# Down projection: feature sums split in the first round, differences ahead of low parts, one square per chunk, and an earlier copy of the row sums

## What is computed

```python
merged = ga * (ya @ w_branch_a[i]) + gb * (yb @ w_branch_b[i]) + gc * (yc @ w_branch_c[i])
x = x + rms_norm(merged @ w_out[i], g_mix_post[i])
h2 = rms_norm(x, g_ffn_pre[i])
u = causal_dwconv(h2 @ w_up[i], conv_w[i], conv_b[i])
ug, uv = u[..., :D_FF], u[..., D_FF:]
f = (jax.nn.gelu(ug, approximate=True) * uv) @ w_down[i]
x = x + rms_norm(f, g_ffn_post[i])
pg = jax.nn.sigmoid(rms_norm(x, g_ple_pre[i]) @ w_ple_gate[i])
x = x + rms_norm(pg * (p[i] @ w_ple[i]), g_ple_post[i])
```

## Time and profile before

| | |
|---|---|
| median of 3 runs | 1868.92 us (1868.49 to 1871.56) |
| the profiled execution | 1870.65 us, its span 1868.8 us |
| PE, matmuls | 1825.6 us busy, 98% of the span |
| DVE | 1175.5 us, 63% |
| ACT | 935.3 us, 50% |
| POOL | 320.6 us, 17% |
| granted clock of PE, mean | 0.989 of full |
| HBM read and written | 145 GB/s over the span |

### The profile page before, as it was taken

How to read it: one execution, slowest core, us unless ns; L and a number is a source line. 1 busy time by engine, 2 the same in 40 slices (tenths; PEclk the granted TensorE clock), 3 DMA queues, 4 the chain that set the end, 5 groups by cost and what they waited for, 6 DMA issues and landing times.

```text
span 1868.8 us, 26896 instructions
## 1 busy us (share of the span) xinstructions
PE 1825.6 (98%) x9111; PEld 1511.3 (81%) x9111; DVE 1175.5 (63%) x1804; ACT 935.3 (50%) x1660; POOL 320.6 (17%) x314
## 2 busy tenths in 40 slices
PE   9999999999999999898999999999989999999988
PEld 8888888787888888776898888887878888887777
DVE  4756555544577777777656555555436777778775
ACT  4676546632454444454547764565235444444453
POOL 1002001232013333101010020012310233331010
PEclk9999999999999999998999999999999999999999
DMA  6322354478323333675253234446762333337742
GB/s 182 83 83 80 108 103 128 115 197 225 102 88 117 107 118 107 226 263 168 93 152 92 58 91 108 96 130 150 196 202 80 110 107 115 118 118 234 249 148 90
DMA packets 311144, 249.23 MB, mean 133 GB/s; under 512 B 65092, under 2 KB 265440, under 8 KB 310752
## 3 DMA queue, kind: packets, MB, share of 16 engines
q1 hardware_dynamic: 301160, 222.51, 39.8%
q0 software_dynamic: 9504, 25.17, 6.3%
q10 hardware_dynamic: 376, 0.21, 0.1%
HBM read 232.57 MB, written 38.27 MB: 145 GB/s over the span
## 4 chain that ended last, share of the span: by engine, by line
PE 61%; DVE 13%; issue 9%; ACT 7%; DMA 6%; POOL 1%; ACTq 1%; DVEq 1%; POOLq 0%; SPq 0%
PE psum L886 51%; DMA col_sums<-in_w_down_dram 4%; ACT wh L1512 3%; PE psum L1201 2%; DVE cg L2428 2%; PE psum L1182 2%; DVE cg L2430 2%; PE psum L1167 2%; ACT cg L1740 2%; DVE ft_both L2430 2%; DVE ft_both L2428 2%; DVE ft_both L2437 2%; DMA row_sums<-in_w_down_dram 1%; ACT ft_both L1740 1%; PE psum L929 1%
## 5 line engine op out<-in xcount | busy, mean ns | idle before, releaser
L886 PE MATMUL psum<-xnh,wh 128*128 128x512 f32 (+1 forms) x1424 | 566.2, 398 | 0.0
L886 PE MATMUL psum<-xnh,wl 128*128 128x512 f32 (+1 forms) x1424 | 549.5, 386 | 0.0
L886 PE MATMUL psum<-xnl,wh 128*128 128x512 f32 (+1 forms) x1424 | 548.8, 385 | 0.0
L1968 DVE TENSOR_TENSOR wl<-raw,wh 128x1024 fp32r<-128x1024 f32 (+2 forms) x276 | 368.7, 1337 | 237.5 <-ACT wh L1512 237.3
L1512 ACT ACTIVATE wh<-raw 128x1024 fp32r<-128x1024 f32 (+2 forms) x276 | 283.2, 1026 | 235.3 <-PE psum L886 178.6
L886 PEld LDWEIGHTS psum<-xnh,wh 128*128 128x128 f32 x1424 | 269.2, 189 | 54.7 <-issue 5.8
L886 PEld LDWEIGHTS psum<-xnh,wl 128*128 128x128 f32 x1424 | 267.7, 188 | 54.6
L886 PEld LDWEIGHTS psum<-xnl,wh 128*128 128x128 f32 x1424 | 268.5, 189 | 46.1
L2203 DVE CUSTOM_DVE_ANT_0 Sp<-psum,ptok 128x128 f32<-128x128 f32 (+3 forms) x128 | 62.7, 491 | 108.6 <-issue 60.8
L1744 ACT ACTIVATE cg<-cg 128x512 f32<-128x512 f32 x44 | 27.8, 633 | 128.7 <-DVE cg L2430 128.7
L1748 ACT ACTIVATE fh<-ft_both 128x256 f32 (+1 forms) x44 | 18.4, 418 | 143.8 <-DVE ft_both L2437 143.8
(11 more groups left out here) (333 smaller groups left out, 3500.3 us busy)
## 6 DMA issues: line engine op xcount, KB each, us to landing
raw<-in_w_up_dram SPq DMA_DIRECT2D x88, 512.0 KB, 3.8
raw<-in_w_gate_dram SPq DMA_DIRECT2D x48, 512.0 KB, 3.8
col_sums<-in_w_down_dram POOLq DMA_DIRECT2D x44, 512.0 KB, 7.0
raw<-in_w_down_dram SPq DMA_DIRECT2D x44, 512.0 KB, 4.5
raw<-in_w_in_dram SPq DMA_DIRECT2D x30, 512.0 KB, 3.7
raw<-col_sums SPq DMA_DIRECT2D x22, 512.0 KB, 4.6
raw<-in_w_down_dram SPq DMA_DIRECT2D x40, 256.0 KB, 4.0
qspill<-f_sums SPq DMA_DIRECT2D x22, 384.0 KB, 4.8
```

The lines of the kernel that those rows point to most:

```text
L886: ins = pe.matmul(out, left, right, start=start and n == 0, stop=stop and n == 2)
L1968: dve.tensor_tensor(low[:, 0:n], raw[(L * NCH + c) % RAW][:, 0:n], hi[:, 0:n].bitcast(F32), ALU.subtract).then_inc(w_lo.sem, 1)
```

## The change

It has five parts. The eleven feature sums are split in the first round (`Q_PREP` 5 to 21) through four buffers that lie where the normed input of the up stage was. In the second round `diff` is made one chunk earlier, in front of the low part of `dn_cols`. Chunk 3's parts are made ahead of the last features, and chunk 4's high part ahead of the last cross features. The sums of squares are taken one at a time, at chunks 31, 33, 35 and 37, and the gains at 30, 32, 34 and 36. The copy of the row sums is issued at POOL's turn 0, with its own semaphore `row_copied`.

```diff
-Q_PREP = [2 * j + 8 for j in range(7)] + [26, 28, 30, 32]
+Q_PREP = [5, 7, 9, 10, 12, 13, 15, 16, 18, 19, 21]
+Q_RAW = 4
...
-    q_raw = [here(f"q_raw{i}", 96 + 3 * i, [P, 768]) for i in range(3)]
+    q_raw = [in_xn(f"q_raw{i}", 16 + 3 * i, [P, 768]) for i in range(Q_RAW)]
... SP
                     if c == ST_DOWN + Q_PREP[j]:
                         if j == 0:
-                            wait(f_lo.sem, f_lo.at(L, 3 * PAIRS))
-                        wait(q_spilled.sem, q_spilled.at(L, 16 * PAIRS) if j == 0 else q_spilled.at(L, 16 * (j + 1)))
-                        if j >= 3:
-                            wait(q_lo.sem, q_lo.at(L, j - 2))
-                        sp.dma_start(q_raw[j % 3][:, :], qspill[L, :, j, :]).then_inc(q_back[j % 3].sem, 16)
-                if c == ST_DOWN + 30:
+                            wait(w_used.sem, w_used.at(L, ST_DOWN))
+                        wait(q_spilled.sem, q_spilled.at(L, 16 * (j + 1)))
+                        if j >= Q_RAW:
+                            wait(q_lo.sem, q_lo.at(L, j - Q_RAW + 1))
+                        sp.dma_start(q_raw[j % Q_RAW][:, :], qspill[L, :, j, :]).then_inc(q_back[j % Q_RAW].sem, 16)
+                if c == ST_DOWN + 28:
                     wait(w_used.sem, w_used.at(L, ST_DOWN + 2 * PAIRS))
                     gain_load(L, 1, "g_ffn_post")
... ACT
+                if last:
+                    hi(L, ST_DOWN + 3)
                 act.wait_ge(ft_ready.sem, ft_ready.at(L, s // 2 + 1) + it * 2)
...
-            act.wait_ge(w_used.sem, w_used.at(L, ST_DOWN + 2 * j + 2))
-            act.activation(qh[:, j, :], q_raw[j % 3][:, :], ACT.Copy).then_inc(q_hi.sem, 1)
+            act.wait_ge(w_used.sem, w_used.at(L, ST_DOWN + 2 * ((3 * j + 2) // 4) + 2))
+            act.activation(qh[:, j, :], q_raw[j % Q_RAW][:, :], ACT.Copy).then_inc(q_hi.sem, 1)
...
-            for n in range(3, 4 * PAIRS + 2):
+            for n in range(5, 4 * PAIRS + 2):
                 hi(L, ST_DOWN + n)
...
-                if n == 31:
-                    half_sums(L)
+                if n in (31, 33, 35, 37):
+                    half_sum(L, n // 2 - 15)
...
-            up_post(L, -1, 2 * FT // 4)
+            up_post(L, -1, 2 * FT // 4, last=True)
+            hi(L, ST_DOWN + 4)
             cross_hi(L, PAIRS - 1)
... DVE
+            if a == 0:
+                dve.wait_ge(q_lo.sem, q_lo.at(L, PAIRS))
             dve.wait_ge(p_full.sem, p_full.at(L, 4 + a))
...
+                dve.wait_ge(p_taken.sem, p_taken.at(L, 4))
             dve.tensor_tensor(yg_dn[:, t, cols], ydn[:, t, cols], gain_down[:, cols], ALU.mult)
...
-            for n in range(3, 4 * PAIRS):
+            for n in range(4, 4 * PAIRS):
                 q = n - 2 * PAIRS
-                if q >= 0 and q % 2 == 1:
+                if q >= 0 and q % 2 == 0:
                     diff(L, q // 2)
...
-                if n in (33, 34, 35, 36):
-                    half_gain(L, n - 33)
+                if n in (30, 32, 34, 36):
+                    half_gain(L, n // 2 - 15)
...
                 lo(L, ST_DOWN + 1)
                 lo(L, ST_DOWN + 2)
+                lo(L, ST_DOWN + 3)
... POOL
-            if s > 0:
+            if s == 0:
+                pool.dma_start(row_sums[L], rows[L, 0, :, 0:1]).then_inc(row_copied.sem, 16)
+            if 0 < s <= PAIRS:
                 pool.wait_ge(wsum_copied.sem, wsum_copied.at(L, 16 * s))
-            if 0 < s <= PAIRS:
                 pool.dma_start(col_sums[L, :, pair(s - 1), :], cols[L, 1, :, pair(s - 1), :], max_dma_last_dim=2048,
                                accum_op=ALU.add).then_inc(wsum_in.sem, 16)
             if s == PAIRS + 1:
+                pool.wait_ge(row_copied.sem, row_copied.at(L, 16))
                 pool.dma_start(row_sums[L], rows[L, 1, :, 0:1], max_dma_last_dim=4096, accum_op=ALU.add
                                ).then_inc(wsum_in.sem, 16)
             if s < PAIRS:
                 pool.dma_start(col_sums[L, :, pair(s), :], cols[L, 0, :, pair(s), :]).then_inc(wsum_copied.sem, 16)
-            if s == PAIRS:
-                pool.dma_start(row_sums[L], rows[L, 0, :, 0:1]).then_inc(wsum_copied.sem, 16)
```

More of the change, by code:

```diff
@@ L361, in trunk_kernel @@
     q_spilled = Tally(sem("q_spilled"), 16 * PAIRS, 16)
-    q_back = [Tally(sem(f"q_back{i}"), 16 * len(range(i, PAIRS, 3))) for i in range(3)]
+    q_back = [Tally(sem(f"q_back{i}"), 16 * len(range(i, PAIRS, Q_RAW))) for i in range(Q_RAW)]
     q_hi = Tally(sem("q_hi"), PAIRS)
     q_lo = Tally(sem("q_lo"), PAIRS)
-    wsum_copied = Tally(sem("wsum_copied"), 16 * (PAIRS + 1))
+    wsum_copied = Tally(sem("wsum_copied"), 16 * PAIRS)
+    row_copied = Tally(sem("row_copied"), 16)
     wsum_in = Tally(sem("wsum_in"), 16 * (PAIRS + 1))
@@ L1728, in keys_apart, with up_post @@
             act.activation(kB[0:HD, 2 * j + 1, :], keys_at[j][HD:P, :], ACT.Copy).then_inc(kt_empty.sem, 1)
-        def up_post(L, s, it):
+        def up_post(L, s, it, last=False):
             value, pair = s % 2, (s // 2) % 2
@@ L1757, in sums_hi @@
         def sums_hi(L, j):
-            act.wait_ge(q_back[j % 3].sem, q_back[j % 3].at(L, 16 * (j // 3 + 1)))
-            act.wait_ge(w_used.sem, w_used.at(L, ST_DOWN + 2 * j + 2))
-            act.activation(qh[:, j, :], q_raw[j % 3][:, :], ACT.Copy).then_inc(q_hi.sem, 1)
+            act.wait_ge(q_back[j % Q_RAW].sem, q_back[j % Q_RAW].at(L, 16 * (j // Q_RAW + 1)))
+            act.wait_ge(w_used.sem, w_used.at(L, ST_DOWN + 2 * ((3 * j + 2) // 4) + 2))
+            act.activation(qh[:, j, :], q_raw[j % Q_RAW][:, :], ACT.Copy).then_inc(q_hi.sem, 1)
         def products_out(L):
@@ L1771, in products_out, with half_sum @@
                     act.activation(dst[a][:, :], bank[4 + 2 * k + a], ACT.Copy).then_inc(p_out.sem, 1)
-        def half_sums(L):
-            for i, t in enumerate((0, 1, 2, 3)):
-                act.wait_ge(half_made.sem, half_made.at(L, i + 1))
-                act.wait_ge(half_summed.sem, half_summed.at(L, i))
-                act.activation(sq_dn[0][:, early_half(t)], ydn[:, t, early_half(t)], ACT.Square, scale=YSCALE,
-                               accum_out=ysums[:, 0, t:t + 1]).then_inc(half_summed.sem, 1)
+        def half_sum(L, t):
+            act.wait_ge(half_made.sem, half_made.at(L, t + 1))
+            act.wait_ge(half_summed.sem, half_summed.at(L, t))
+            act.activation(sq_dn[0][:, early_half(t)], ydn[:, t, early_half(t)], ACT.Square, scale=YSCALE,
+                           accum_out=ysums[:, 0, t:t + 1]).then_inc(half_summed.sem, 1)
         def rest_sum(L, i):
@@ L2058, in sums_lo @@
             dve.wait_ge(q_hi.sem, q_hi.at(L, j + 1))
-            dve.tensor_tensor(ql[:, j, :], q_raw[j % 3][:, :], qh[:, j, :].bitcast(F32), ALU.subtract
+            dve.tensor_tensor(ql[:, j, :], q_raw[j % Q_RAW][:, :], qh[:, j, :].bitcast(F32), ALU.subtract
                               ).then_inc(q_lo.sem, 1)
         def threes_taken(L, a):
+            if a == 0:
+                dve.wait_ge(q_lo.sem, q_lo.at(L, PAIRS))
             dve.wait_ge(p_full.sem, p_full.at(L, 4 + a))
```

## The result

The changed kernel takes 1841.76 us, the median of four executions (1841.51 to 1847.50), beside 1869.76 (1868.49 to 1871.56) for the kernel before on the same chip: a ratio of 0.9857, 95% interval 0.9836 to 0.9878. That is 28.0 us less where 38.5 were forecast. The time lies inside the range of 1822 to 1846, but 11.4 us above the forecast of 1830.4 (the kernel before had 1868.92 when the forecast was made), so outside the 5 us around it. The profiled execution of the changed kernel is the slowest of its four: 1847.5 us, span 1845.7. Its span is 23.1 us under that of the profile before.

What follows compares the result with a forecast made beforehand. TensorE (PE) was taken as the bound, busy in 98% of the span. Gains of 14.1 us at the gates, 11.5 in layer 0 and 12.9 in layer 1 made 38.5 off 1868.92: 1830.4 us, range 1822 to 1846.

Steps and rivals of the forecast that it cites:

- (a): First round of down: the loads hold it, landing in 7.2 us; 5.9 us a layer, 1842 in all; chance 0.17.
- (b): Second round of down: it loses through the difference's wait, landings 5.7 us; 5.4 a layer, 1841 in all; chance 0.09.
- the gates: End of the third branch's gates: issuing the row_sums copy at POOL's turn 0 gains 14.1 us, low end 10.
- one of its own signs: Down projection: the prediction is wrong if row sums wait for DMA in most pairs, or if diffs do.
- Turn 11 still waits for the copy of pair 10: POOL's queue at the gates: that copy had landed by 437.15, and PE stood nowhere for it.
- chunk 3 and chunk 4: First round: the 3.33 us stall before chunk 3 goes; a new one of 1.4 us comes before chunk 4.
- From there PE eats a pair in 5.44 us: First round after chunk 4: DVE needs 4.5 us per pair, under PE's 5.44, so no loss.
- the 2.9 of the prediction: First round: loss left in the round, 1.4 + 1.5 us, of 6.2 and 6.6 before.
- three causes that the prediction named: Second round: four fewer low parts of sums on DVE, squares spread out, difference one chunk ahead (0.76 us waited before).
- Low 39 ended T-3.4, load 43 lands T+1.4: Second round's tail, T being when PE ends chunk 37: leads to a 1.9 us stall and 0.2 to restart.
- cycle over two pairs: Second round: DVE's loads and parts take 7.1 to 7.7 us, under PE's 8.16, so no loss.
- the embedding's give-back: Embedding after down: DVE's last additions start later, so 1.8 us a layer comes back as a PE stall.

Runs made afterwards that it cites:

- the yardstick's: The changed kernel run once more without any edit, in the second group, beside the kernel before: 1843.38 us, ratio 0.9857.

## Why the prediction was right, and where it was wrong

The time lies in the range, but near the rivals (a) and (b), at 1842 and 1841 us, and not near the forecast. It is not there for their reasons in full, as shown below: the gates came as forecast, the down projection gained much less, and the embedding's error went the other way and hid 4.7 us of that, which is luck. By one of its own signs the prediction failed: it was to be wrong if differences wait for their loads, and 8 of 11 do in each layer. The row sums do so in 4 and 5 of 10.

**Right: the gates, by mechanism and size.** 14.1 us forecast; 12.6 measured alone. In the profiled execution of the changed kernel 4.4 of them came back in layer 1 through the copy of pair 9; in the yardstick's trace nothing did. The three executions with spans near 1840 are 5.8 us shorter than the profiled one; that this stall is most of what they lack is argued from its size, as they have no trace. The slow matmuls in the first rounds (3.2 us in the profiled execution, none in the yardstick's trace) are another thing that comes and goes. "Turn 11 still waits for the copy of pair 10" was true, but the wait at pair 9 was not looked at in the prediction, and the profile before had left it no effect.

**Right: chunk 3 and chunk 4.** The stall before chunk 3 went as forecast, and chunk 4 loses 0.83 and 0.81 us where 1.4 stood. It is not all new: the profile before shows 1.02 us lost before chunk 4 in layer 0 (769.35), which the prediction did not name.

**Wrong in the first round: the step "From there PE eats a pair in 5.44 us. DVE needs ..., 4.5 us per pair".** It takes undisturbed durations and an average over 17 chunks. The stall that came, 1.98 us at chunk 6, lies right at its beginning, where the first sum's low part (1.49) stands ahead of low 6, and where POOL's last two low parts still slow DVE. The prediction had that slowing down for chunk 4 and dropped it from there on. Two runs show it: with POOL quiet 0.36 is left, with the sum moved nothing is. Behind it a second thing was hidden, SP's spill ahead of loads 8 and 9; with both out of the way the rounds lose 2.5 us each, near the 2.9 of the prediction. Rival (a) is not this: DVE's row sums did wait for loads, PE was not held by them.

**Right in sign, too large in the second round: the regular part.** PE stands nowhere between the rounds' change and chunk 38, as forecast, in the first trace; in the yardstick's it stands 1.54 us once, for a load of 7.7 us. Of the three causes that the prediction named, the difference ahead of time is worth 4.0 to 5.7 us by medians of different groups, of which the trace shows 2.6 as stalls of the ping-pong. The spread squares are worth nothing that can be measured once the rest is in place: the 3.31 us that DVE stood for high 32 would have been filled by a wait for a load. What the four low parts fewer are worth was not tried alone.

**Wrong in the tail: the step "Low 39 ended T-3.4, load 43 lands T+1.4".** T was 844.3. Low 39 ended at 842.65, T-1.7, because load 39, issued at 835.05, landed at 840.2, and each difference now waits for its load. Load 43 then took 5.06 us where 4.8 stood, and landed at T+3.5, not T+1.4. The mis-sized term stands ahead of it, the "cycle over two pairs" of 7.1 to 7.7 us: from one difference to the second after it DVE needed 7.6 to 8.3 us in the last pairs of layer 0 (828.37 to 836.10 is 7.73, 831.93 to 840.22 is 8.29) and 8.0 to 8.6 in layer 1, beside PE's 8.16. So the parts gained nothing on PE on the way, and in the tail three pairs fall due at once. Thus 1.9 us became 0.77 and 3.20, and 2.26 and 3.48 in layer 1, with 1.7 to 1.9 more at the slow clock. That is the tail of rival (b), with its "1.9 if the clock falls there", and at 3.6 and 5.7 us a layer over the forecast it is near (b)'s 5.4. But (b)'s condition, landings of 5.7 us, holds only in part: the loads from 33 on took 4.4 to 5.2 us in layer 0 and 4.9 to 6.0 in layer 1 (load 43 there 6.04), and its 1.5 us in the pairs did not come in this trace.

**Wrong with it: the embedding's give-back.** The 1.8 us per layer needed a PE that is early. As PE is late in the tail, the cover holds and the embedding loses 0.0 and 0.5. Once PE is made earlier, by the shorter tail or the buffers, it loses 3.9 to 7.0 us a layer there, two to four times what was forecast. The mechanism was right, its size too small.

Summed: the gates gained 4.4 us, the first rounds 6.3 and the second rounds 9.4 less than forecast, the embedding 4.7 more: 15.4 less in all for the profiled execution. The median is 11.4 off; that it is less goes with the stall at the gates, which the profiled execution has and the others probably lack. In the yardstick's trace the same account reads otherwise: gates as forecast, first rounds 3.1 and second rounds 14.0 less, embedding 5.2 more. That the second rounds hold most of the miss stands in both.

In two versions every execution is under every one of the changed kernel's, in both of its groups: the later spill with the later split (1840.20), and the one with two more buffers on top of it (1840.17). The first changes a list and one number and is the one to take. It is 3.2 us under the changed kernel of its own group, or 0.2%.

## What to carry to other kernels

When stalls are removed from one engine, ask of each remaining wait on the helpers whether it only becomes visible next: here ping-pong with ACT turned into waits for loads. What the shorter tail or the buffers took off the tail came back in the embedding or at another load, and no version tried here won both. An average rate of work per pair is no proof for the first pairs: work out the first and the last ones one by one, with the durations that hold while the other engines are still busy. And an in-order queue that waits for a slow producer, as SP's spill did, holds the urgent loads behind it; put the transfer that nobody needs soon behind them.

## What was not expected of the hardware

The same standstill of PE did not cost the same each time. Before chunk 6 of layer 0 PE stood 1.98 us in the first trace and 1.97 in the yardstick's, behind the same work. In the first, matmuls from 767.98 on start 0.43 us apart, the lower of the clock's two levels (1.2 of 2.4 GHz), for about 3.3 us, and the window's granted clock is 0.97; in the second they go on at the full pitch and it is 1.00. That is 1.6 us between two executions of one program with the same stall. The same stall stands in both layers of six traces, 12 times: in 7 of them the first round loses 6.0 us, in 5 it loses 4.4 to 4.5. What decides it no run here shows.

The same load of 512 KB, issued at the same place of the round, took 5.7 us in one execution of the changed kernel and 7.7 in another. PE's loss in that round was 5.7 and 10.2 us, of which 1.54 lie behind this load. Differences under 4 us in one profiled round are not to be put down to an edit here without a stall that shows it.
